# A fused two-layer block: the feed-forward's gate/up products rotate through six accumulator banks instead of eight, with three spare buffers instead of four

## The chip, the core and the metric

The kernel runs on one core of a Trainium2 chip. A core has TensorE (PE) for matrix products, VectorE (DVE), ScalarE (ACT) and GpSimd (POOL) for the rest, and SyncE (SP), whose queue issues the loads from HBM. They work side by side and wait for each other on semaphores. PE writes only to PSUM, an accumulator memory of 8 banks of 128 partitions by 512 float32 values; DVE and ACT read it from there. The metric is the device time of one execution in microseconds (us); less is better. Three executions of the kernel before took 1556.65, 1557.42 and 1561.18 us.

## The reference

A first block (gated delta rule and windowed attention, 256 tokens of width 1024) is followed by a second one of two layers. Each of these layers is a feed-forward, a mixer, and another feed-forward, each with its own modulated norm and gate:

```python
D_FF = 2816; HALF_STEP = 0.5

def _swiglu(h, w_gate, w_up, w_down):
    return (jax.nn.silu(h @ w_gate) * (h @ w_up)) @ w_down

for l in range(DEPTH_2):                                   # 2 layers
    mod = jax.nn.silu(c) @ w_mod[l] + b_mod[l]
    sh1, sc1, g1, sh2, sc2, g2, sh3, sc3, g3 = jnp.split(mod[:, None, :], N_MOD, axis=-1)
    h = _rmsnorm_2(x) * (1.0 + sc1) + sh1
    x = x + HALF_STEP * g1 * _swiglu(h, ffn1_w_gate[l], ffn1_w_up[l], ffn1_w_down[l])
    h = _rmsnorm_2(x) * (1.0 + sc2) + sh2
    x = x + g2 * _hybrid_mixer(h, w_in[l], w_out[l], ...)
    h = _rmsnorm_2(x) * (1.0 + sc3) + sh3
    x = x + HALF_STEP * g3 * _swiglu(h, ffn2_w_gate[l], ffn2_w_up[l], ffn2_w_down[l])
```

All is float32. The change touches the four feed-forwards and the places where they meet their neighbours.

## The kernel before

The program is written out by hand, engine by engine (`tensor_program`, `vector_program`, and so on). Nothing reorders it: each engine runs its list in order, and a `wait_ge(key)` stands where a step needs another's result. `Lane.wait_ge` leaves out a wait that an earlier one on the same engine already covers, since a semaphore only counts up.

**The feed-forward.** The four are called by (layer, sub): (0,0), (0,2), (1,0), (1,2). The hidden width of 2816 is 22 column blocks of 128, called f or x; they are taken in 11 pairs, which I number 0 to 10. For the precision, each float32 operand is split in a rounded high part and a low rest, and each product is the sum of high x high, high x low and low x high. A pair runs in four quarters q: gate weights with the first four slices of the model width, gate weights with the other four, then the same with the up weights. In each quarter PE does first the column block j = 0 of the pair, then j = 1 (`pe_ffn`). For each slice there is one product of 512 columns (`ps<-hh,whi`: the high weights against the high and low input side by side) and one of 256 (`ps<-hh,wlo`). A column block accumulates in two PSUM banks, one for gate and one for up, so a pair uses four banks. They are taken at q = 0, two when j = 0 begins and two when j = 1 begins, by `pe.bank(key, "ga")`.

**The banks.** `Tensor.bank` hands out the banks of a named pool in turn, and makes PE wait until the last holder of that bank is free. `POOLS` lists the pools: "ga" for gate/up, "down" for the four accumulators of the down product, "turnf" and "turnx" for the normed input that PE turns ahead of a block ("turnf" ahead of both mixers and of (1,0), "turnx" ahead of the others), "outx" for the mixer's output, "proj" (0, 1) and "rec" (2, 3) for the start of the mixer. The turn of "ga" is set back to 0 at the start of each feed-forward; with eight banks the even pairs use 0 to 3 and the odd ones 4 to 7.

**After the products.** When a column block is complete, ACT copies half of the two banks to a spare buffer (L2057, `copied`), DVE adds the other half (L2108, `summed`), and with that the two banks are free. ACT makes the Silu (L2060), DVE multiplies (L2113), ACT rounds the high part (L2064, `ahi`), POOL takes the low rest (L2076, `alo`). The spare buffers `SG` are the right halves of `H`, four of them, used in turn. In between ACT and DVE split the weight pieces of the next pair (L2026 `whi`, L2087 `wlo`); a piece can only be split when PE has done the piece four before it. In `split_all` the pieces of the next pair's quarters 0, 1 and 2 come ahead of the work on the finished pair, that of quarter 3 behind it.

**Beside it.** In the feed-forwards DVE also computes the modulation vectors of later stages: products with the vector c over tiles of 128 x 1024, summed (L555, `v_mods`), placed by `beside` and `along`. There is much of it in the first three feed-forwards and little in the last.

**The down product** takes its four banks all at once, before its first matmul, and then runs 22 slices of 12 matmuls. Then `v_join` scales by the gate, adds to x, and frees the banks; the norm and the turn-in of the next stage follow.

Of the kernel before, what the change touches and what calls it, by code (L numbers as in the profile page):

```python
# [107 lines left out]
ALU, ACT, AX = mybir.AluOpType, mybir.ActivationFunctionType, mybir.AxisListType  # L108
# [104 lines left out]
def plain(a):  # L213
    return a.bitcast(f32)


NS = 5
POOLS = {"all": range(8), "crow": (0, 1), "ccol": (2, 3), "tx": (4, 5, 6, 7), "six": range(6), "mods": (6, 7), "rest": (0, 1), "att": (2, 3, 4, 5), "bo": (7,), "sq": (4, 5, 6, 7), "low": (0, 1), "skk": (2,), "sdec": (4, 5), "sq2": (6, 7), "ga": range(8),
         "down": (4, 5, 6, 7), "chain": (2, 3, 4, 5), "proj": (0, 1), "rec": (2, 3), "sd": (4, 5, 6), "dbo": (7,), "outx": (2, 3, 0, 1), "ds": (4, 5, 6, 7), "turnf": (0, 1, 2, 3), "turnx": (6, 7, 4, 5)}


class Store:
# [203 lines left out]
class Tensor(Lane):  # L426
# [6 lines left out]
    def bank(self, key, pool="all"):  # L433
        banks = POOLS[pool]
        i = self.turn.get(pool, 0)
        self.turn[pool] = i + 1
        b = banks[i % len(banks)]
        if b in self.held:
            self.wait_ge(("free", self.held[b]))
        self.held[b] = key  # L440
        self.M.banks[key] = b
        return self.M.psum[:, b, :]
# [1482 lines left out]


def spare(M):
    return [M.H[:, 2 * i:2 * i + 2, 256:512] for i in range(4)]


def piece(M, i, n):

    return [t[:, i % 4, :].rearrange("p (a b) -> p a b", b=n) for t in (M.WHI, M.WLO)]


def pieces(l, sub):

    out, n = [], 0
    for f in range(0, 22, 2):
        for i in range(2):  # L1940
            for h in range(2):
                out.append((n, ("fw", l, sub, f, i), 4 * h, 4, 256, h == 1))
                n += 1
    for k0 in range(0, 22, 2):
        for h in range(2):
            out.append((n, ("out", ("d", l, sub), k0), h, 1, 1024, h == 1))
            n += 1
    return out
# [72 lines left out]
def act_piece(a, l, sub, p):  # L2021
    M = a.M
    n, key, r0, rn, wd_, _ = p
    hi, _ = piece(M, n, wd_)
    a.wait_ge(key, ("staged", l, sub, n - 4))
    a.done(a.e.activation(hi, M.slot(key)[:, r0:r0 + rn, :], ACT.Copy), ("whi", l, sub, n))  # L2026


def act_ffn(a, l, sub):
    M = a.M  # L2030
    SG = spare(M)

    def emit(p):
        act_piece(a, l, sub, p)

    def high(blk, half):
        k, t = slice(4 * half, 4 * half + 4), slice(blk * 128, blk * 128 + 128)
        a.wait_ge(("h", l, sub, blk, half))
        a.done(a.e.activation(M.HHI[:, k, t], M.H[:, k, t], ACT.Copy), ("hhi", l, sub, blk, half))

    first = pieces(l, sub)[:4]
    high(0, 0)
    act_modulated(a, l, sub, 0)
    high(0, 1)
    emit(first[1])
    high(1, 0)
    act_modulated(a, l, sub, 1)
    high(1, 1)
    for p in first[2:]:
        emit(p)  # L2050
    for f in split_all(a, l, sub, emit, None):
        pair = range(f, f + 2) if isinstance(f, int) else ()
        for x in pair:
            key = ("gu", l, sub, x)
            b = M.banks[key, 0]
            a.wait_ge(key, ("alo", l, sub, x - 4))
            a.done(a.e.activation(SG[x % 4], M.psum[:, b:b + 2, 256:512], ACT.Copy), ("copied", l, sub, x))  # L2057
        for x in pair:
            a.wait_ge(("summed", l, sub, x))
            a.done(a.e.activation(SG[x % 4][:, 0, :], SG[x % 4][:, 0, :], ACT.Silu), ("silu", l, sub, x))  # L2060
        for j, x in enumerate(pair):
            i = x % 4
            a.wait_ge(("act", l, sub, f + j))
            a.done(a.e.activation(M.AHI[:, f + j, :], SG[i][:, 0, :], ACT.Copy), ("ahi", l, sub, f + j))  # L2064


def pool_ffn(g, l, sub):
    M = g.M
    SG = spare(M)
    for half in range(2):  # L2070
        k = slice(4 * half, 4 * half + 4)
        g.wait_ge(("hhi", l, sub, 0, half))
        g.done(g.e.tensor_tensor(M.HLO[:, k, 0:128], M.H[:, k, 0:128], plain(M.HHI[:, k, 0:128]), ALU.subtract), ("hlo", l, sub, half))
    for f in range(22):
        g.wait_ge(("ahi", l, sub, f))
        g.op(g.e.tensor_tensor(M.ALO[:, f, :], SG[f % 4][:, 0, :], plain(M.AHI[:, f, :]), ALU.subtract), ("alo", l, sub, f))  # L2076


def v_ffn(v, l, sub, work):
    M = v.M  # L2080
    SG = spare(M)

    def emit(p):
        n, key, r0, rn, wd_, ends = p
        hi, lo = piece(M, n, wd_)
        v.wait_ge(("whi", l, sub, n), ("staged", l, sub, n - 4))
        v.done(v.e.tensor_tensor(lo, M.slot(key)[:, r0:r0 + rn, :], plain(hi), ALU.subtract), ("split", l, sub, n),  # L2087
             *([M.freed(key)] if ends else []))

    def low(half):  # L2090
        k, t = slice(4 * half, 4 * half + 4), slice(128, 256)
        v.wait_ge(("hhi", l, sub, 1, half))
        v.done(v.e.tensor_tensor(M.HLO[:, k, t], M.H[:, k, t], plain(M.HHI[:, k, t]), ALU.subtract), ("hlo", l, sub, half))  # L2093

    first = pieces(l, sub)[:4]
    emit(first[0])
    v_modulated(v, l, sub, 1)
    low(0)
    emit(first[1])
    low(1)  # L2100
    for p in first[2:]:
        emit(p)
    for f in split_all(v, l, sub, emit, work):
        for j in range(2 if isinstance(f, int) else 0):
            i, key = (f + j) % 4, ("gu", l, sub, f + j)
            b = M.banks[key, 0]
            v.wait_ge(("copied", l, sub, f + j))
            v.done(v.e.tensor_tensor(SG[i], SG[i], M.psum[:, b:b + 2, 0:256], ALU.add), ("summed", l, sub, f + j),  # L2108
                   ("free", (key, 0)), ("free", (key, 1)))
        for j in range(2 if isinstance(f, int) else 0):  # L2110
            i = (f + j) % 4
            v.wait_ge(("silu", l, sub, f + j))
            v.done(v.e.tensor_tensor(SG[i][:, 0, :], SG[i][:, 0, :], SG[i][:, 1, :], ALU.mult), ("act", l, sub, f + j))  # L2113


def pe_ffn(pe, l, sub):
    M = pe.M
    pe.turn["ga"] = 0
    for f in range(0, 22, 2):
        for q in range(4):  # L2120
            n = 2 * f + q
            hi, lo = piece(M, n, 256)
            k0 = 4 * (q % 2)
            pe.wait_ge(("split", l, sub, n), ("hlo", l, sub, q % 2))
            for j in range(2):
                c, key = slice(j * 128, j * 128 + 128), ("gu", l, sub, f + j)
                if q == 0:
                    for i in range(2):
                        pe.bank((key, i), "ga")
                b = M.ps((key, q // 2))  # L2130
                for kt in range(k0, k0 + 4):
                    low = lambda: pe.mm(b[:, 0:256], lo[:, kt - k0, c], M.HHI[:, kt, :], False, False)
                    if kt:
                        low()
                    ins = pe.mm(b, hi[:, kt - k0, c], M.HH[:, :, kt, :], kt == 0, kt == 7)
                    if kt == 0:
                        low()
                if q == 3 and j == 0:
                    pe.done(ins, key)
            pe.done(ins, ("staged", l, sub, n), *([key] if q == 3 else []))  # L2140
    bs = [[pe.bank(("d", l, sub, blk, hf), "down") for hf in range(2)] for blk in range(2)]
    for k0 in range(19):
        part = [k0] if k0 < 18 else [18, 19, 20, 21]
        pe.wait_ge(("alo", l, sub, part[-1]))
        for blk, kt, hf in [(0, k_, h_) for k_ in part for h_ in range(2)] + [(1, k_, h_) for h_ in range(2) for k_ in part]:
            n, c, s = 44 + kt, slice(blk * 128, blk * 128 + 128), slice(hf * 512, hf * 512 + 512)
            hi, lo = piece(M, n, 1024)
            pe.wait_ge(("split", l, sub, n))
            ins = pe.mm3(bs[blk][hf], (M.AHI[:, kt, c], M.ALO[:, kt, c]), (hi[:, 0, s], lo[:, 0, s]), kt == 0, kt == 21)
            if kt == 21 or (blk and hf):  # L2150
                pe.done(ins, *([("staged", l, sub, n)] if blk and hf else []), *([("d", l, sub, blk, hf)] if kt == 21 else []))
# [801 lines left out]
```

## Time and profile before

| | |
|---|---|
| median of three runs | 1557.42 us (1556.65 to 1561.18) |
| the profiled execution's own time | 1561.18 us |
| its span, first to last instruction | 1559.4 us |
| mean granted clock of TensorE | 0.969 of 2.4 GHz |
| busy: PE, DVE, ACT, POOL | 1466.9, 1017.5, 699.6, 298.0 us |
| share of PE in the chain that ended last | 80% |
| instructions | 18939 |

A row of the profile names a line of the kernel, the engine, the operation, and output<-inputs. L445 is `Tensor.mm`, through which all matmuls go, so they are told apart by their tiles: `hh,whi` and `hh,wlo` are gate/up, `whi,ahi`, `wlo,ahi` and `whi,alo` are down. PEld is the load of a matmul's stationary weights, which runs beside the matmul ahead of it. Matmuls overlap in the pipeline, so the distance between two starts is their pace, not their durations. Rows of DVE overlap by 0.08 us in the same manner.

### The profile page before, as it was taken

How to read it: one execution, taken by the hardware profiler on the slowest of the kernel's cores; microseconds unless marked ns; L12 is line 12 of the kernel's file. 1: busy time of each engine (PE TensorE's matmuls, PEld its weight loads, DVE VectorE, ACT ScalarE, POOL GpSimd, SP SyncE). 2: the span in 40 equal slices, each digit the busy share in tenths (PEclk: the TensorE clock that was granted, in tenths of full speed). 3: DMA queues.
4: the chain of work that ended last, by engine and by line, in shares of the span. 5: the costliest groups of instructions: out<-in, count | busy, mean ns of one | idle time of the engine just before them, and what ended most of it. 6: DMA issues, size and time to landing. Idle time of an engine off the chain costs nothing.

```text
span 1559.4 us, 18939 instructions
## 1 busy us (share of the span) xinstructions
PE 1466.9 (94%) x7424; PEld 1129.5 (72%) x7424; DVE 1017.5 (65%) x1531; ACT 699.6 (45%) x1116; POOL 298.0 (19%) x269
## 2 busy tenths in 40 slices
PE   6997999989889999999989999899999999999999
PEld 3546556646678888775578888788887865778887
DVE  4276684852568887346568886688884553776654
ACT  4425321152255653362355654466542631466552
POOL 0321255002211110043221110011100341311100
PEclk8998999998899999999999999999999999999999
DMA  9444234224258889332348988488895413478551
GB/s 384 162 142 139 95 131 179 91 108 149 86 188 294 299 325 365 109 118 94 108 141 283 318 308 317 134 284 293 318 357 167 134 63 108 135 240 260 180 198 55
DMA packets 159641, 306.41 MB, mean 196 GB/s; under 512 B 5952, under 2 KB 115776, under 8 KB 148672
## 3 DMA queue, kind: packets, MB, share of 16 engines
q1 hardware_dynamic: 159120, 304.93, 56.4%
q8 instruction: 58, 0.95, 0.3%
q10 hardware_dynamic: 432, 0.27, 0.1%
q14 instruction: 31, 0.25, 0.1%
HBM read 304.11 MB, written 1.08 MB: 196 GB/s over the span
## 4 chain that ended last, share of the span: by engine, by line
PE 80%; DVE 11%; ACT 6%; issue 1%; POOL 1%; DMA 1%; SPq 0%; DVEq 0%; ACTq 0%
PE ps L445 79%; PE ps L448 1%; DMA ring<-in_w_first_dram 1%; DVE H L1911 1%; DVE arena L1277 1%; DVE arena L1274 1%; ACT arena L1541 1%; DVE H L1860 0%; DVE misc L1574 0%; DVE arena L2726 0%; DVE arena L1263 0%; DVE H L1845 0%; DVE X L1851 0%; POOL arena L2465 0%; DVE ring L555 0%
## 5 line engine op out<-in xcount | busy, mean ns | idle before, releaser
L445 PE MATMUL ps<-hh,whi 128*128 128x512 f32 x1408 | 485.4, 399 | 6.1 <-DVE hh L2093 6.1
L2087 DVE TENSOR_TENSOR wlo<-ring,whi 128x1024 fp32r<-128x1024 f32 x264 | 321.8, 1231 | 149.7 <-ACT whi L2026 147.6
L2026 ACT ACTIVATE whi<-ring 128x1024 fp32r<-128x1024 f32 x264 | 274.2, 1055 | 227.2 <-PE ps L445 210.2
L445 PE MATMUL ps<-hh,wlo 128*128 128x256 f32 x1408 | 366.3, 281 | 0.0
L445 PEld LDWEIGHTS ps<-hh,whi 128*128 128x128 f32 x1408 | 252.9, 189 | 55.6 <-DVE hh L2093 7.0
L445 PEld LDWEIGHTS ps<-hh,wlo 128*128 128x128 f32 x1408 | 266.3, 189 | 16.6
L445 PE MATMUL ps<-ring,H 128*128 128x512 f32 (+1 forms) x544 | 238.4, 590 | 9.2 <-ACT arena L2228 5.6
L445 PEld LDWEIGHTS ps<-ring,H 128*128 128x128 f32 x544 | 104.0, 198 | 116.7 <-issue 101.0
L555 DVE SCALAR_TENSOR_TENSOR ring<-ring,cb 128x1024 f32<-128x1024 f32 x144 | 179.0, 1244 | 4.4 <-DMA ring<-in_mods_dram 4.0
L445 PE MATMUL ps<-H,ring 128*128 128x256 f32 (+1 forms) x576 | 160.1, 437 | 4.9 <-ACT arena L840 3.7
L2076 POOL TENSOR_TENSOR alo<-H,ahi 128x256 fp32r<-128x256 f32 x88 | 70.5, 802 | 460.3 <-ACT ahi L2064 456.8
L445 PEld LDWEIGHTS ps<-arena 128*128 128x128 f32 (+3 forms) x1320 | 124.3, 171 | 36.3 <-issue 21.0
L445 PE MATMUL ps<-arena 128*128 128x64 f32 (+6 forms) x1320 | 138.2, 267 | 10.3 <-DVE arena L1588 7.4
L445 PEld LDWEIGHTS ps<-H,ring 128*128 128x128 f32 x576 | 111.2, 195 | 50.1 <-issue 32.1
L445 PE MATMUL ps<-whi,alo 128*128 128x512 f32 x376 | 145.2, 390 | 0.0
L445 PE MATMUL ps<-wlo,ahi 128*128 128x512 f32 x360 | 140.1, 389 | 0.0
L445 PE MATMUL ps<-whi,ahi 128*128 128x512 f32 x352 | 137.0, 389 | 0.0
L445 PEld LDWEIGHTS ps<-whi,alo 128*128 128x128 f32 x376 | 70.6, 188 | 14.9
L445 PEld LDWEIGHTS ps<-wlo,ahi 128*128 128x128 f32 x360 | 67.6, 188 | 14.2
L445 PEld LDWEIGHTS ps<-whi,ahi 128*128 128x128 f32 x352 | 66.1, 188 | 13.7
L2057 ACT ACTIVATE H<-ps 128x512 f32<-128x512 f32 x88 | 52.8, 600 | 48.6 <-PE ps L445 48.6
L2108 DVE TENSOR_TENSOR H<-H,ps 128x512 f32<-128x512 f32 x88 | 57.8, 680 | 5.0 <-ACT H L2057 3.8
(344 smaller groups left out, 1553.4 us busy)
## 6 DMA issues: line engine op xcount, KB each, us to landing
ring<-in_mods_dram SPq DMA_DIRECT2D x76, 1024.0 KB, 5.6
ring<-in_w_in_dram SPq DMA_DIRECT2D x48, 1024.0 KB, 5.2
ring<-in_ffn_w_gate_dram SPq DMA_DIRECT2D x44, 1024.0 KB, 5.4
ring<-in_ffn_w_up_dram SPq DMA_DIRECT2D x44, 1024.0 KB, 7.1
ring<-in_ffn_w_down_dram SPq DMA_DIRECT2D x44, 1024.0 KB, 6.4
ring<-in_w_out_dram SPq DMA_DIRECT2D x12, 1024.0 KB, 5.0
ring<-in_w_first_dram SPq DMA_DIRECT2D x8, 1024.0 KB, 14.3
gates<-gate_rows SPq DMA_DIRECT2D x7, 512.0 KB, 6.0
```

The costliest lines, as they stand in the source:

```text
L445: return self.e.matmul(o, lhsT, rhs, start=start, stop=stop)
L448: return self.e.transpose(o, in_, self.M.C["ident"])
L555: v.done(v.e.scalar_tensor_tensor(tile, tile, 1.0, M.cvec[p.k], ALU.mult, ALU.mult, accum_out=sums[:, j:j + 1]), ("mod sums", p.n), *([M.f ...
L1274: v.op(v.e.tensor_tensor(t, M.AT[:, k, 0:k].unsqueeze(2).broadcast_to([128, k, w_]), M.XS[:, k, k:32].unsqueeze(1).broadcast_to([128, k, w ...
L1277: v.op(v.e.tensor_tensor(x, x, t, ALU.add))
L1541: a.done(a.e.activation(sm[:, t4, :], sm[:, t4, :], ACT.Exp, bias=nm[:, t4:t4 + 1], accum_out=den[:, t4:t4 + 1]), ("soft", u))
L1911: v.done(v.e.tensor_scalar(M.H[:, k, blk * 128:(blk + 1) * 128], M.ps(key)[:, HS[k]], m[:, cc + k:cc + k + 1], m[:, cs + k:cs + k + 1], AL ...
L2026: a.done(a.e.activation(hi, M.slot(key)[:, r0:r0 + rn, :], ACT.Copy), ("whi", l, sub, n))
L2057: a.done(a.e.activation(SG[x % 4], M.psum[:, b:b + 2, 256:512], ACT.Copy), ("copied", l, sub, x))
L2076: g.op(g.e.tensor_tensor(M.ALO[:, f, :], SG[f % 4][:, 0, :], plain(M.AHI[:, f, :]), ALU.subtract), ("alo", l, sub, f))
L2087: v.done(v.e.tensor_tensor(lo, M.slot(key)[:, r0:r0 + rn, :], plain(hi), ALU.subtract), ("split", l, sub, n), *([M.freed(key)] if ends els ...
L2108: v.done(v.e.tensor_tensor(SG[i], SG[i], M.psum[:, b:b + 2, 0:256], ALU.add), ("summed", l, sub, f + j), ("free", (key, 0)), ("free", (key ...
```

## The change

The pool "ga" has six banks, 0 to 5, and its turn is no longer set back, so that a feed-forward starts where the one before it stopped (a feed-forward takes 44 banks). "down" is (2, 3, 4, 5) instead of (4, 5, 6, 7). "turnf" is (6, 7, 0, 1) instead of (0, 1, 2, 3). The spare buffers are three, and ACT's copy of block x waits for the low part of x - 3.

```diff
--- before.py
+++ after.py
@@ -215,8 +215,8 @@
 
 
 NS = 5
-POOLS = {"all": range(8), "crow": (0, 1), "ccol": (2, 3), "tx": (4, 5, 6, 7), "six": range(6), "mods": (6, 7), "rest": (0, 1), "att": (2, 3, 4, 5), "bo": (7,), "sq": (4, 5, 6, 7), "low": (0, 1), "skk": (2,), "sdec": (4, 5), "sq2": (6, 7), "ga": range(8),
-         "down": (4, 5, 6, 7), "chain": (2, 3, 4, 5), "proj": (0, 1), "rec": (2, 3), "sd": (4, 5, 6), "dbo": (7,), "outx": (2, 3, 0, 1), "ds": (4, 5, 6, 7), "turnf": (0, 1, 2, 3), "turnx": (6, 7, 4, 5)}
+POOLS = {"all": range(8), "crow": (0, 1), "ccol": (2, 3), "tx": (4, 5, 6, 7), "six": range(6), "mods": (6, 7), "rest": (0, 1), "att": (2, 3, 4, 5), "bo": (7,), "sq": (4, 5, 6, 7), "low": (0, 1), "skk": (2,), "sdec": (4, 5), "sq2": (6, 7), "ga": range(6),
+         "down": (2, 3, 4, 5), "chain": (2, 3, 4, 5), "proj": (0, 1), "rec": (2, 3), "sd": (4, 5, 6), "dbo": (7,), "outx": (2, 3, 0, 1), "ds": (4, 5, 6, 7), "turnf": (6, 7, 0, 1), "turnx": (6, 7, 4, 5)}
 
 
 class Store:
@@ -1925,7 +1925,7 @@
 
 
 def spare(M):
-    return [M.H[:, 2 * i:2 * i + 2, 256:512] for i in range(4)]
+    return [M.H[:, 2 * i:2 * i + 2, 256:512] for i in range(3)]
 
 
 def piece(M, i, n):
@@ -2053,13 +2053,13 @@
         for x in pair:
             key = ("gu", l, sub, x)
             b = M.banks[key, 0]
-            a.wait_ge(key, ("alo", l, sub, x - 4))
-            a.done(a.e.activation(SG[x % 4], M.psum[:, b:b + 2, 256:512], ACT.Copy), ("copied", l, sub, x))
+            a.wait_ge(key, ("alo", l, sub, x - 3))
+            a.done(a.e.activation(SG[x % 3], M.psum[:, b:b + 2, 256:512], ACT.Copy), ("copied", l, sub, x))
         for x in pair:
             a.wait_ge(("summed", l, sub, x))
-            a.done(a.e.activation(SG[x % 4][:, 0, :], SG[x % 4][:, 0, :], ACT.Silu), ("silu", l, sub, x))
+            a.done(a.e.activation(SG[x % 3][:, 0, :], SG[x % 3][:, 0, :], ACT.Silu), ("silu", l, sub, x))
         for j, x in enumerate(pair):
-            i = x % 4
+            i = x % 3
             a.wait_ge(("act", l, sub, f + j))
             a.done(a.e.activation(M.AHI[:, f + j, :], SG[i][:, 0, :], ACT.Copy), ("ahi", l, sub, f + j))
 
@@ -2073,7 +2073,7 @@
         g.done(g.e.tensor_tensor(M.HLO[:, k, 0:128], M.H[:, k, 0:128], plain(M.HHI[:, k, 0:128]), ALU.subtract), ("hlo", l, sub, half))
     for f in range(22):
         g.wait_ge(("ahi", l, sub, f))
-        g.op(g.e.tensor_tensor(M.ALO[:, f, :], SG[f % 4][:, 0, :], plain(M.AHI[:, f, :]), ALU.subtract), ("alo", l, sub, f))
+        g.op(g.e.tensor_tensor(M.ALO[:, f, :], SG[f % 3][:, 0, :], plain(M.AHI[:, f, :]), ALU.subtract), ("alo", l, sub, f))
 
 
 def v_ffn(v, l, sub, work):
@@ -2102,20 +2102,19 @@
         emit(p)
     for f in split_all(v, l, sub, emit, work):
         for j in range(2 if isinstance(f, int) else 0):
-            i, key = (f + j) % 4, ("gu", l, sub, f + j)
+            i, key = (f + j) % 3, ("gu", l, sub, f + j)
             b = M.banks[key, 0]
             v.wait_ge(("copied", l, sub, f + j))
             v.done(v.e.tensor_tensor(SG[i], SG[i], M.psum[:, b:b + 2, 0:256], ALU.add), ("summed", l, sub, f + j),
                    ("free", (key, 0)), ("free", (key, 1)))
         for j in range(2 if isinstance(f, int) else 0):
-            i = (f + j) % 4
+            i = (f + j) % 3
             v.wait_ge(("silu", l, sub, f + j))
             v.done(v.e.tensor_tensor(SG[i][:, 0, :], SG[i][:, 0, :], SG[i][:, 1, :], ALU.mult), ("act", l, sub, f + j))
 
 
 def pe_ffn(pe, l, sub):
     M = pe.M
-    pe.turn["ga"] = 0
     for f in range(0, 22, 2):
         for q in range(4):
             n = 2 * f + q
```

The instructions on each engine and their order stay the same, and only what they wait for changes. The first place is PE in (0,0), at the start of the gate/up products of pair 1; the names are the input's high and low parts (`hh`) and the weights' high and low parts (`whi`, `wlo`). Before:

```order
L445 MATMUL ps<-hh,whi 128x512 [waits s_act_done,s_dve_done]
L445 MATMUL ps<-hh,wlo 128x256 x2
L445 MATMUL ps<-hh,whi 128x512
L445 MATMUL ps<-hh,wlo 128x256
L445 MATMUL ps<-hh,whi 128x512
L445 MATMUL ps<-hh,wlo 128x256
L445 MATMUL ps<-hh,whi 128x512 x2
L445 MATMUL ps<-hh,wlo 128x256 x2
```

The same rows after the change:

```order
L445 MATMUL ps<-hh,whi 128x512 [waits s_act_done,s_dve_done]
L445 MATMUL ps<-hh,wlo 128x256 x2
L445 MATMUL ps<-hh,whi 128x512
L445 MATMUL ps<-hh,wlo 128x256
L445 MATMUL ps<-hh,whi 128x512
L445 MATMUL ps<-hh,wlo 128x256
L445 MATMUL ps<-hh,whi 128x512
L445 MATMUL ps<-hh,whi 128x512 [waits s_dve_done]
L445 MATMUL ps<-hh,wlo 128x256 x2
```

The first matmul of column block j = 1 of the pair now waits for DVE. Before, there was no wait at that place: the next one came with the second quarter.

The second place is PE in (0,2), from the end of the first slice of the down product to the beginning of the second (`ahi`, `alo`: the hidden activations). Before:

```order
L445 MATMUL ps<-wlo,ahi 128x512
L445 MATMUL ps<-whi,alo 128x512
L445 MATMUL ps<-whi,ahi 128x512 [waits s_dve_done,s_pool_done]
L445 MATMUL ps<-wlo,ahi 128x512
L445 MATMUL ps<-whi,alo 128x512
```

The same rows after the change:

```order
L445 MATMUL ps<-wlo,ahi 128x512
L445 MATMUL ps<-whi,alo 128x512
L445 MATMUL ps<-whi,ahi 128x512 [waits s_pool_done]
L445 MATMUL ps<-wlo,ahi 128x512
L445 MATMUL ps<-whi,alo 128x512
```

The second slice doesn't wait for DVE any more, because the wait in front of the first slice (for the banks) is now for a later step of DVE, which covers the split of the second slice's weights too.

## Rows read from the trace of the kernel before

**Rows 1.** The page: busy time by engine, and POOL's low parts.
```profile
PE 1466.9 (94%) x7424; PEld 1129.5 (72%) x7424; DVE 1017.5 (65%) x1531; ACT 699.6 (45%) x1116; POOL 298.0 (19%) x269
...
L2076 POOL TENSOR_TENSOR alo<-H,ahi 128x256 fp32r<-128x256 f32 x88 | 70.5, 802 | 460.3 <-ACT ahi L2064 456.8
```

**Rows 2.** The chain of waits: start, us, what; first and last feed-forward.
```profile
446.67 184.27 PE ps L445 x962
...
1371.41 184.10 PE ps L445 x968
```

**Rows 3.** Windows: us, busy by engine (PE, PEld, DVE, ACT, POOL), granted clock, DMA.
```profile
446.70:571.00 124.30, 124.30 (x698) 107.94 (x699) 103.65 (x142) 75.53 (x109) 14.79 (x20) 0.99 0.84 289
...
700.00:716.00 16.00, 13.59 (x76) 9.57 (x75) 12.60 (x15) 6.51 (x10) 8.48 (x7) 1.00 0.38 129
806.00:811.00 5.00, 3.40 (x16) 3.21 (x16) 3.27 (x7) 2.98 (x6) 2.17 (x2) 0.66 0.43 150
1371.40:1495.00 123.60, 123.59 (x702) 107.39 (x703) 84.89 (x104) 74.16 (x109) 14.76 (x20) 1.00 0.70 229
```

**Rows 4.** Timeline (start, us), all engines, end of (0,0)'s last pair.
```profile
572.00 0.19 PEld L445 LDWEIGHTS ps<-whi,ahi 128*128 128x128 f32 x1
572.23 0.40 PE L445 MATMUL ps<-whi,ahi 128*128 128x512 f32 x1
...
572.43 0.60 ACT L2057 ACTIVATE H<-ps 128x512 f32<-128x512 f32 x1 [0.82 <-PE ps L445]
...
573.05 1.28 DVE L2108 TENSOR_TENSOR H<-H,ps 128x512 f32<-128x512 f32 x2
```

**Rows 5.** Timeline, all engines, from (0,0)'s pair 9 into pair 10.
```profile
561.17 0.60 ACT L2057 ACTIVATE H<-ps 128x512 f32<-128x512 f32 x1 [0.82 <-PE ps L445]
561.19 1.30 DVE L2108 TENSOR_TENSOR H<-H,ps 128x512 f32<-128x512 f32 x2
...
562.02 0.30 PEld L445 LDWEIGHTS ps<-hh,whi 128*128 128x128 f32 x2
562.13 0.62 PE L445 MATMUL ps<-hh,whi 128*128 128x512 f32 x2
...
562.86 0.42 ACT L2064 ACTIVATE ahi<-H 128x256 fp32r<-128x256 f32 x1
```

**Rows 6.** Timeline, all engines, start of (0,0)'s gate/up products.
```profile
445.92 0.69 DVE L2093 TENSOR_TENSOR hh<-H,hh 128x512 fp32r<-128x512 f32 x1 [0.69 <-ACT hh L2039]
...
446.67 0.19 PEld L445 LDWEIGHTS ps<-hh,whi 128*128 128x128 f32 x1 [2.14 <-DVE hh L2093]
446.67 0.50 PE L445 MATMUL ps<-hh,whi 128*128 128x512 f32 x1 [1.95 <-DVE hh L2093]
446.77 0.42 PEld L445 LDWEIGHTS ps<-hh,wlo 128*128 128x128 f32 x2
```

**Rows 7.** Timeline, DVE and ACT, first and last pair with late additions.
```profile
458.10 1.23 DVE L2087 TENSOR_TENSOR wlo<-ring,whi 128x1024 fp32r<-128x1024 f32 x1 [1.63 <-ACT whi L2026]
...
459.77 0.60 ACT L2057 ACTIVATE H<-ps 128x512 f32<-128x512 f32 x1 [0.82 <-PE ps L445]
...
460.38 1.28 DVE L2108 TENSOR_TENSOR H<-H,ps 128x512 f32<-128x512 f32 x2
...
1405.51 0.60 ACT L2057 ACTIVATE H<-ps 128x512 f32<-128x512 f32 x1 [0.82 <-PE ps L445]
...
1406.13 1.27 DVE L2108 TENSOR_TENSOR H<-H,ps 128x512 f32<-128x512 f32 x2
```

**Rows 8.** Timeline, ACT and DVE, last pairs of (1,0) and (1,2).
```profile
1129.73 0.60 ACT L2057 ACTIVATE H<-ps 128x512 f32<-128x512 f32 x1 [0.82 <-PE ps L445]
...
1130.35 1.28 DVE L2108 TENSOR_TENSOR H<-H,ps 128x512 f32<-128x512 f32 x2
...
1495.12 0.68 DVE L2108 TENSOR_TENSOR H<-H,ps 128x512 f32<-128x512 f32 x1
...
1495.64 0.60 ACT L2057 ACTIVATE H<-ps 128x512 f32<-128x512 f32 x1 [0.82 <-PE ps L445]
```


## The prediction

> **What bounds the kernel now.** I read the page first: TensorE (PE) is busy for 1466.9 of 1559.4 us, and no other engine comes near it [rows 1]. Then the chain of waits, where the reader is to see one thing: each of the four feed-forward blocks is a single unbroken piece of PE work. The first runs for 184.27 us from 446.67, the last for 184.10 us from 1371.41 [rows 2], and the two between them look the same. Together that is some 737 us with nothing in between, so a stall of PE inside a block is added to the end in full, and no idle time exists there that could give it back. The windows by stage say the same: PE is busy for 124.30 of 124.30 us in the first gate/up half and for 123.59 of 123.60 in the last, at granted clock 0.99 and 1.00 [rows 3].
>
> Then the timeline around the place where a pair of blocks of the hidden width ends, since the change moves the waits there. I write E for the start of the second ACT copy of a pair (L2057, waits for PE's last matmul of the pair). In the last pair of (0,0), E is 572.43. PE goes on without a gap: the weight load of the first down matmul is at 572.00 and the matmul at 572.23, so E - 0.43 and E - 0.20 [rows 4]. One pair earlier E is 561.17, 11.26 us before. Half a quarter later PE turns to the second column block of the next pair; the two weight loads in a row mark it (562.02 and 562.13) and the second of the two matmuls in a row, at 562.37: so E + 0.96 and E + 1.20 [rows 5].
>
> **The change part by part.**
>
> *The six-bank ring.* A pair takes four banks. With eight banks a pair needs those of the pair two before it, freed long ago. With six, the first block of a pair takes banks of the pair before last, but the second block takes the two that the first block of the pair just finished has held. So once per pair PE must wait, at E + 0.96, for DVE's addition to that block (L2108, "summed"), and this wait stood nowhere near the path before. When is the addition done? DVE's row x2 holds both additions of a pair; a single one takes 0.68 us [rows 8], so the first one is over 0.68 us after the row's start.
> - In the pair that ends at 572.43 the row starts at 573.05 (`v_ffn` runs a modulation product, L555, just ahead of it): over at 573.73, E + 1.30 [rows 4].
> - In the pair that ends at 561.17 it starts at 561.19: over at E + 0.70 [rows 5], 0.26 us before the weight load is due. No stall.
> - In the last feed-forward block, once the modulation work has run out, it is over at E + 0.16 [rows 8]. No stall.
>
> The late kind is every second pair of the first three blocks (pairs 0, 2, 4, 6, 8) and pairs 0 and 2 of the last: 17 pairs, the first with E 459.77 and the row at 460.38, the last with E 1405.51 and the row at 1406.13, both E + 0.61 + 0.68 = E + 1.29 to 1.30 [rows 7]. It doesn't get less late when PE has been held up: the DVE row that opens its chain sat idle for 1.63 us for ACT's rounded weight piece, which itself waits for PE's third quarter of the same pair [rows 7]. So the lateness moves along with PE and is paid each time.
>
> What does a wait cost that ends late? At the start of the feed-forward block DVE's row ends at 446.61; weight load and matmul begin at 446.67, and with the next weight load at 446.77 the first matmul streams from there [rows 6]. So streaming starts 0.15 us after the end of the awaited row. A late pair: E + 1.30 + 0.15 against E + 1.20, 0.25 us. 17 x 0.25 = 4.3 us. The trace has no wait of PE in mid-stream that just misses, so this is bounded: from below 0.10 us less (the weight load not held by the wait), 0.15 us, 2.6 us in all; from above 0.23 us more (a further weight load that can't run ahead, the 0.23 between load and matmul in rows 4), 0.48 us, 8.2 us in all. I take 0.25, the row nearest in kind. Below nothing is excluded, since PE has no idle time in these stretches.
>
> *The down banks and the ring without a reset.* A block takes 44 banks, 44 mod 6 is 2, so the four blocks start at banks 0, 2, 4 and 0. Down now takes banks 2 to 5 at once, before its first matmul. In (0,0) and (1,2) the last pair holds 4, 5 (first column block) and 0, 1: down waits for the first addition. In (0,2) and (1,0) its second column block holds 2, 3 and 4, 5: down waits for the second addition. Before, down had 4 to 7, held by the pair before. The matmul was due at E - 0.20:
> - (0,0): E + 1.30 + 0.15 + 0.20 = 1.65 us [rows 4].
> - (0,2) and (1,0): the second addition is over at 1131.63 with E at 1129.73, so E + 1.90 [rows 8]; 1.90 + 0.35 = 2.25 us each. The pairs of (0,2) have the same rhythm.
> - (1,2): the first addition is over at 1495.80, E 1495.64 [rows 8]; 0.16 + 0.35 = 0.51 us.
>
> Sum 6.7 us; by the same bounds (0.10 less, 0.23 more, four times) 6.3 to 7.6.
>
> *Three spare buffers instead of four.* ACT's copy of block x now waits for the low part of x - 3, not x - 4. For the first of a pair that lies two pairs back, for the second in the first half of the pair before. ACT rounds the first block of a pair at 562.86, E + 1.69 [rows 5], and POOL's 0.80 us [rows 1] follow; the copy that now waits comes 9.8 us after E. Nothing; if that cover were gone, a delay of ACT would first eat the slack of the additions above.
>
> *Turn-in banks.* The mixers and (1,0) now turn in to 6, 7, 0, 1. 6 and 7 are idle in the gate/up half and 0, 1 are freed by its last pairs at the latest, a whole down product earlier. The mixer's first projections take bank 0 and 1, now held by the second row block's turn-in; but they need that block's modulated rows anyway. Nothing. No instruction is added, removed or put elsewhere on any engine, DMAs included.
>
> The sum: 4.3 + 6.7 = 11.0 us. The profiled execution has span 1559.4 and time 1561.18; with the change 1570.4 and 1572.2. The median of the runs shown, 1557.42, lies 3.8 us under the profiled one, so the forecast of the median is 1557.4 + 11.0 = 1568.4.
>
> **The rivals.** A measurement of this kernel can tell about 0.3% (4.7 us) from no change: up to 1562.1 counts as the same.
>
> *Only the four down starts cost.* If the late additions in mid-block are taken up (DVE's row ends are no release times, and the gap to cover is 0.25 us), 6.7 us stay: 1564.1. For it: the miss is small. Against it: the weight load is due at E + 0.96, and the addition only starts at E + 0.61 and has 0.68 us to run.
>
> *The clock falls.* Stalls of 2 us in the middle of a dense stream could bring PE to its lower level, 1.2 GHz. In 806 to 811, after a join in which PE sat idle at several places, the granted clock is 0.66: 5 x 0.34 / 0.5 = 3.4 us at half speed. If that followed each of four down starts, PE at half speed for 3.4 us would lose 1.7 us each time: 6.8 more, 1575.2. Against it: from 700 to 716 PE is busy for 13.59 of 16.00 us, idle for 2.41, more than any stall forecast here, and the clock stays at 1.00 [rows 3]. The Trainium skill, "TensorE: Matmul & The Clock Gate", section "A second HAM failure mode: psum-queue depth-cycling", speaks for this rival: a kernel that cycled through its PSUM banks idled so often in short gaps between groups that the clock went back and forth, at a cost in throughput though single matmuls looked alike. By that rule, with gaps at each late pair too, the time would lie at this rival's or above; this trace shows no such case, as its ring never stalled.
>
> *The waits are hidden.* The change does in the program what it says, but if PE's waits for the additions released by other means (the row ends being late by 2 us) it would give 1557.4.
>
> *Faster.* PE spends 11.26 us on a pair of 32 matmuls of 512 and 32 of 256 columns; at 2.4 GHz these columns are 10.24 us. The other 1.02 us a pair, 45 us over 44 pairs, could be a collision of PE's reads with what ACT and DVE move in SBUF and PSUM. If the smaller set of banks and buffers took a third of it away, 15 us, the time would be 1557.4 + 11.0 - 15 = 1553.4; it decides from 11.0 us, a pair under 11.01 us between stalls. Against it: the excess doesn't depend on that traffic. The first block's gate/up half has DVE busy for 103.65 us and the last one's for 84.89, with DMA shares 0.84 and 0.70 [rows 3], and the blocks take 184.27 and 184.10 us [rows 2].
>
> **How the numbers follow.** Forecast 0.64; only the down starts 0.16; clock 0.08; hidden 0.07; faster 0.05. The predicted time is the forecast's, 1568.4. Its own range is 8.9 to 15.8 us over the median, 1566.3 to 1573.2. Low end of the range: the down starts alone with 2 us of scatter, 1562. High end: 1574. Slower by over 0.3%: 0.64 + 0.08 + most of 0.16 = 0.85. Same: 0.07 and the rest, 0.10. Faster: 0.05.
>
> **What would show it.** In the profile after: (a) PE rows with idle time before them, released by DVE L2108 (the addition), some 17 of 0.2 to 0.5 us at E + 0.96 in mid-pair, in every second pair, and four at the first down matmul, about 1.6, 2.2, 2.2 and 0.5 us; (b) the three middle blocks' pieces in the chain broken by ACT and DVE, and the blocks 187.2, 187.6, 187.6 and 185.1 us long; (c) mixers and joins unchanged; (d) clock 1.00 in the blocks. The forecast is wrong if the PE rows wait for the additions but resume sooner than 0.15 us, if odd pairs stall as well (then 0.26 us of slack was no slack), or if the clock in the blocks falls under 0.98.

## The result, and the profile after

The changed kernel takes 1571.41 us (median of 4 runs, 1570.06 to 1571.86) against 1558.26 for the kernel before beside it: 13.2 us slower, ratio 1.0088, 95% interval 1.0072 to 1.0105. The forecast was 11.0 us slower, 1568.4. (One execution of the kernel before, beside later runs, took 1706.64 us at a granted clock of 0.823; no comparison here uses it.) The profiled execution has a span of 1573.8 us, 14.4 over the 1559.4 of before. By the page's first line PE is busy for 6.9 us more, its weight loads for 3.1, and the others for the same within 0.7:

```profile
PE 1473.8 (94%) x7424; PEld 1132.6 (72%) x7424; DVE 1018.1 (65%) x1531; ACT 699.0 (44%) x1116; POOL 297.8 (19%) x269
```

The view of waits shows where the time went. PE's matmul rows waited five times for DVE's addition (L2108), but the rows of the weight loads did so 21 times; in the kernel before neither did once:

```profile
PE ps L445 <- DVE H L2108: 5.9, 5, 2.0
...
PEld ps L445 <- DVE H L2108: 12.4, 21, 2.3
```

21 is 17 + 4. Why the matmul rows show so few is seen in the timeline (all engines) of a late pair, (0,0)'s pair 0, which answers to [rows 7] and [rows 5]:

```profile
459.82 0.60 ACT L2057 ACTIVATE H<-ps 128x512 f32<-128x512 f32 x1 [0.82 <-PE ps L445]
...
460.44 1.28 DVE L2108 TENSOR_TENSOR H<-H,ps 128x512 f32<-128x512 f32 x2
...
460.79 0.89 PE L445 MATMUL ps<-hh,whi 128*128 128x512 f32 x2
...
461.18 0.19 PEld L445 LDWEIGHTS ps<-hh,whi 128*128 128x128 f32 x1 [0.31 <-DVE H L2108]
461.29 0.42 PEld L445 LDWEIGHTS ps<-hh,wlo 128*128 128x128 f32 x2
461.52 0.40 PE L445 MATMUL ps<-hh,wlo 128*128 128x256 f32 x2
```

E is 459.82. The addition is over at 460.44 + 0.68 = 461.12, and the load starts 0.06 us later, at 461.18, where it was due at 460.78. The matmuls of 512 columns are drawn as one row of 0.89 us (0.62 in [rows 5]), since their ends are modelled: the hole is in there. Start to start tells it: 461.52 less 460.79 is 0.73, where the same stretch before took 0.47 (460.73 to 461.20).

The end of (0,0)'s last pair, as in [rows 4] (timeline, all engines):

```profile
573.75 0.60 ACT L2057 ACTIVATE H<-ps 128x512 f32<-128x512 f32 x1 [0.81 <-PE ps L445]
...
574.37 1.28 DVE L2108 TENSOR_TENSOR H<-H,ps 128x512 f32<-128x512 f32 x2
...
575.11 0.19 PEld L445 LDWEIGHTS ps<-whi,ahi 128*128 128x128 f32 x1 [1.72 <-DVE H L2108]
575.11 0.50 PE L445 MATMUL ps<-whi,ahi 128*128 128x512 f32 x1 [1.40 <-DVE H L2108]
```

The chain of waits, one piece from 446.67 before [rows 2], is broken there, and shows what sets the addition's time (start, us, what):

```profile
446.75 124.15 PE ps L445 x688
...
570.99 1.07 ACT whi L2026
...
572.08 1.23 DVE wlo L2087
573.31 1.14 DVE ring L555 x2
574.45 0.61 DVE H L2108
...
575.11 58.79 PE ps L445 x258
```

PE's third quarter releases ACT's rounding, this DVE's rest, then comes the modulation product, then the addition. The chain leaves the block's matmuls at 633.90, six before the last, as it did before: 187.15 us against 184.27, forecast 187.2.

In (0,2) something more is to be seen. PE's rows at the start of down (timeline):

```profile
942.00 0.50 PE L445 MATMUL ps<-whi,ahi 128*128 128x512 f32 x1 [1.99 <-DVE H L2108]
942.33 0.39 PE L445 MATMUL ps<-wlo,ahi 128*128 128x512 f32 x1
942.56 0.47 PE L445 MATMUL ps<-whi,alo 128*128 128x512 f32 x1
942.83 0.63 PE L445 MATMUL ps<-whi,ahi 128*128 128x512 f32 x1
943.26 0.63 PE L445 MATMUL ps<-wlo,ahi 128*128 128x512 f32 x1
943.69 0.63 PE L445 MATMUL ps<-whi,alo 128*128 128x512 f32 x1
```

From 942.83 on the starts are 0.43 us apart instead of 0.23: PE is at its lower clock. The windows (columns as in [rows 3]; the granted clock is third from the end) show it behind the stalls of (0,2) and (1,0), at the start of (1,0), and not in the last block (the start of (0,0), not shown, has it in both kernels):

```profile
942.70:946.20 3.50, 3.50 (x10) 2.69 (x9) 2.67 (x4) 1.39 (x3) 3.25 (x2) 0.51 0.18 53
1013.50:1018.00 4.50, 4.43 (x14) 3.85 (x15) 4.02 (x5) 3.21 (x5) 0.00 (x0) 0.52 0.55 167
1144.10:1147.60 3.50, 3.50 (x10) 2.75 (x9) 2.01 (x3) 1.28 (x2) 2.81 (x2) 0.51 0.51 130
1384.70:1509.00 124.30, 124.27 (x703) 107.54 (x704) 85.11 (x105) 74.14 (x109) 14.75 (x20) 1.00 0.69 228
```

**The sum of the profiled execution**, from the distances between matmul starts. Of each block I take first gate/up start to last down start; without a stall and at full clock that is 183.7 us.

| block | before | after | mid-pair waits | down start | rest |
|---|---|---|---|---|---|
| (0,0) | 185.2 | 188.1 | 1.27 | 1.66 | 1.5 |
| (0,2) | 183.7 | 188.9 | 1.46 | 2.25 | 1.5 |
| (1,0) | 183.7 | 190.5 | 1.27 | 2.30 | 3.3 |
| (1,2) | 183.7 | 184.7 | 0.50 | 0.51 | 0.0 |
| all | 736.4 | 752.3 | 4.50 | 6.7 | 6.2 |

The waits are 11.2 us. The rest is the lower clock: matmul starts 0.43 us apart. The kernel before has 1.5 us of it in its blocks, this one 6.2. 11.2 + 4.7 is 15.9; outside the blocks the execution lost 1.5 us less than that of before, which makes the 14.4.

### The profile page after: what moved, and what is told of

Its sections match the earlier page's. It is cut to its first block, busy times and chain, and to the rows that moved or that the text cites. A ratio compares the mean times of both kernels' runs of the same rounds, so it can differ in the third digit from the quotient of the medians.

```text
span 1573.8 us, 18934 instructions
## 1 busy us (share of the span) xinstructions
PE 1473.8 (94%) x7424; PEld 1132.6 (72%) x7424; DVE 1018.1 (65%) x1531; ACT 699.0 (44%) x1116; POOL 297.8 (19%) x269
## 4 chain that ended last, share of the span: by engine, by line
PE 77%; DVE 12%; ACT 6%; DMA 2%; issue 2%; POOL 1%; SPq 0%; DVEq 0%; ACTq 0%
PE ps L445 76%; PE ps L448 1%; DMA ring<-in_w_first_dram 1%; DVE H L1911 1%; DVE ring L555 1%; DVE arena L1277 1%; DVE arena L1274 1%; DMA ring<-in_ffn_w_gate_dram 1%; DVE wlo L2087 1%; ACT arena L1541 1%; ACT whi L2026 0%; DVE H L1860 0%; DVE misc L1574 0%; DVE H L2108 0%; DVE arena L2725 0%
## 5 line engine op out<-in xcount | busy, mean ns | idle before, releaser
L445 PE MATMUL ps<-hh,whi 128*128 128x512 f32 x1408 | 490.8, 401 | 5.9 <-DVE hh L2093 5.7
L2108 DVE TENSOR_TENSOR H<-H,ps 128x512 f32<-128x512 f32 x88 | 58.2, 682 | 7.8 <-ACT H L2057 7.4
## 6 DMA issues: line engine op xcount, KB each, us to landing
ring<-in_w_first_dram SPq DMA_DIRECT2D x8, 1024.0 KB, 13.5
```

What stands on the lines that cost most here:

```text
L445: return self.e.matmul(o, lhsT, rhs, start=start, stop=stop)
```

## The experiments

Theory W: the time is PE's waits for the additions, plus what the clock does. Rivals: the spare buffers or turn-in banks cost something; six banks cost something by themselves. Differences are medians against the kernel before on the same chip; where a diff is against the changed kernel it says so. `POOLS` entries are shown alone.

**Spares and turn-in banks alone.** The changed kernel, with the ring and down as before:

```diff
-"ga": range(6)   "down": (2, 3, 4, 5)
+"ga": range(8)   "down": (4, 5, 6, 7)
 def pe_ffn(pe, l, sub):
+    pe.turn["ga"] = 0
```

> The three spare buffers and the new turn-in banks alone; gate/up keeps eight banks with the reset, down keeps 4 to 7. Theory W (the time is made of PE's waits for DVE's additions and of what the clock does after them): no wait is added on PE, 0 us, within 0.3% of the kernel before; the four blocks 185.2, 183.7, 183.7, 183.7 us from first gate/up matmul to last down matmul, as before. Rival S (the fourth buffer's loss delays ACT's copies, or the turn-in banks hold up the mixers): 2 us or more slower, with ACT's copy row waiting for POOL.

1560.49 against 1561.20 us, ratio 0.9994 (0.9984 to 1.0004); no load or matmul waits for L2108, and three of the four blocks take 183.6 to 183.7 us (the fourth, 185.0, has the lower clock at its start). These two parts add no wait, and rival S, 2 us or more, falls.

**Only the mid-pair waits.** The changed kernel, with

```diff
-"down": (2, 3, 4, 5)
+"down": (6, 7, 2, 3)
 def pe_ffn(pe, l, sub):
+    pe.turn["ga"] = 0
```

> The whole change, but the ring starts at bank 0 in each block and down takes 6, 7, 2, 3, which are free by then: only the mid-pair waits stay. Theory W: 17 late pairs at 0.25 us, 4.3 us slower than before (about 1562.5 if before is 1558.3), no half-clock stretch inside a block. Rival (the mid-pair waits cost little and the down starts make the 13 us): under 2 us slower. Rival (short gaps in mid-block also bring the clock down): over 8 us slower, with matmul starts 427 ns apart after some of them.

1566.80 against 1561.20: 5.6 us, ratio 1.0043 (1.0029 to 1.0058). The waits of its profile:

```profile
PEld ps L445 <- DVE H L2108: 5.3, 17, 0.3
```

Seventeen, and by matmul starts they cost 4.3 us: 0.145 us until the late matmul and 0.10 at the next, 0.25 each, as Theory W has it. The median lies above that, the interval from 4.5 to 9.1 us; the profile has 2.1 us of lower clock at the start of (0,2). There is no lower clock in mid-block: the 17 short holes didn't bring it down here.

**Only down starts, on the second addition.** The kernel before, with

```diff
-"down": (4, 5, 6, 7)
+"down": (2, 3, 4, 5)
```

> The kernel before, with down on banks 2 to 5: each of the four down starts waits for the second addition of the last pair, no other wait is added. Theory W with the clock: four stalls of 2.25, 2.25, 2.25 us and, in the last block, 1.33 + 0.35 = 1.7 us, 8.4 us together, and behind each of the three long ones a stretch at 1.2 GHz that costs 1.7 us, 5.1 us: 13.5 us slower. Theory W without the clock (what the profile of the changed kernel shows of it is chance): 8.4 us slower.

1570.88 against 1561.20: 9.7 us, ratio 1.0062 (1.0046 to 1.0079). Four waits:

```profile
PEld ps L445 <- DVE H L2108: 8.7, 4, 2.3
```

By starts they cost 2.25, 2.25, 2.25 and 1.67 us, 8.4 as forecast. The windows behind the first and the third of the stalls, alike in length:

```profile
571.90:576.00 4.10, 4.10 (x18) 3.40 (x19) 3.19 (x5) 3.09 (x5) 3.18 (x2) 1.00 0.33 93
...
1136.70:1140.30 3.60, 3.55 (x9) 2.80 (x10) 3.17 (x5) 2.12 (x4) 2.60 (x2) 0.53 0.42 98
```

The same stall left the clock at 1.00 once and brought it to 0.53 once. So the clock doesn't answer every stall of 2.2 us, and it does so in other kernels than the changed one too. The median, 9.7, lies between the theory's two numbers.

**Only down starts, on the first addition.** The kernel before, with

```diff
-"down": (4, 5, 6, 7)
+"down": (0, 1, 4, 5)
```

> The kernel before, with down on banks 0, 1, 4, 5: each down start waits for the first addition of the last pair. Theory W: stalls of 1.65 us three times and 0.51 us, 5.5 us slower. If the clock falls only behind the longer stalls, as in (0,2) and (1,0) of the changed kernel and not in its (0,0), no more than that; if it falls behind these too, 1.7 us for each of three, 10.6 us slower.

1564.94 against 1561.20: 3.7 us, ratio 1.0022 (1.0011 to 1.0033).

```profile
PEld ps L445 <- DVE H L2108: 5.7, 4, 1.7
```

The stalls cost 1.65, 1.65, 1.66 and 0.50 us in the profile, 5.5 as forecast; the median came out 1.8 lower, its interval just short of it. The clock behind them is 1.00, (0,0) shown:

```profile
573.90:577.00 3.10, 3.10 (x14) 2.55 (x14) 2.66 (x6) 2.53 (x5) 1.62 (x1) 1.00 0.37 152
```

**The changed kernel again.**

> The changed kernel once more, beside three variants of it. Theory W: 11.0 us of waits, plus a stretch at 1.2 GHz worth 1.7 us behind those of the two stalls of 2.2 us (down starts of (0,2) and (1,0)) that the clock happens to answer: between 11 and 14.4 us slower than before. If such a stretch stood behind both stalls in every execution, always 14.4; in the run that broke the stalls apart (down on banks 2 to 5), one of three stalls of 2.2 us was followed by one.

1572.72 against 1559.50: 13.2 us, ratio 1.0084 (1.0072 to 1.0097). Its profile has 4.5 + 6.7 us of waits again, half-clock stretches behind both stalls of 2.2 us again, and none at the start of (1,0): 4.6 us of lower clock in the blocks instead of 6.2.

**The ring set back.** The changed kernel, with

```diff
 def pe_ffn(pe, l, sub):
     M = pe.M
+    pe.turn["ga"] = 0
```

> The changed kernel with the ring set back to bank 0 in each block, so that every down start waits for the first addition of the last pair, none for the second. Theory W: 4.3 us in mid-pair as before, and 1.65, 1.65, 1.65 and 0.51 us at the down starts, 5.5 us: 9.7 us slower than the kernel before, 1.2 us and the clock's share (up to 3.4) less than the changed kernel; no stretch of matmul starts 427 ns apart behind a down start. Rival (the clock falls by chance behind any down stall): the stretches stay and the time is within 1 us of the changed kernel's.

> The changed kernel with the ring set back, again: its first five rounds gave 13.9 us over the kernel before where its waits are worth 9.7. Theory C: 9.3 to 9.8 us of waits in the profile again, the rest half-clock stretches at block starts, in another number than the three of its first profile; median between 9.7 and 15 us over before. Rival (a cost of the reset itself): the same blocks longer by the same amount.

1573.44 against 1559.50 and, again, 1571.78 against 1559.68: 13.9 and 12.1 us, ratios 1.0092 (1.0077 to 1.0107) and 1.0084 (1.0065 to 1.0103). The waits are as forecast in both, 9.8 and 9.9 us, and no stretch at the lower clock follows a down start. But the gain on the changed kernel that Theory W promised doesn't show in the medians: the first is within 1 us of the changed kernel's beside it, as the rival had it, though the stretches that the rival needed aren't there. The lower clock is at the block starts instead. Windows of the first 5 us of (0,2), in the first and in the second profile:

```profile
812.50:817.90 5.40, 5.40 (x19) 4.63 (x20) 4.10 (x4) 3.25 (x6) 0.00 (x0) 0.57 0.58 194
```

```profile
812.60:817.90 5.30, 5.30 (x30) 4.67 (x31) 4.81 (x5) 4.18 (x6) 0.00 (x0) 1.00 0.54 195
```

The first profile has it at the starts of (0,0), (0,2) and (1,0), 5.1 us, the second at those of (0,0) and (1,2), 3.1 us: it differs between executions of one program.

**The kernel before again.**

> The kernel before once more, for a second profile of it. Theory C (where the half-clock stretches behind the joins fall against the starts of the feed-forward blocks differs from one execution to the next, and each that reaches into a block costs 1 to 2 us there): the blocks are 183.7 us but for 0 to 2 of the four, which are 1 to 2 us longer at their start; the granted clock in mid-block is 1.00 throughout. Rival (such stretches come with the changed code alone): the same single one, at (0,0), as in the first profile.

1559.18 against 1559.68. One block of four has the stretch, now (1,0) and not (0,0):

```profile
444.90:450.00 5.10, 5.10 (x30) 4.46 (x31) 4.61 (x5) 4.13 (x6) 0.00 (x0) 1.00 0.59 196
...
1001.70:1007.00 5.30, 5.30 (x22) 4.59 (x23) 4.04 (x4) 3.79 (x6) 0.00 (x0) 0.68 0.58 198
```

That fits Theory C. What it leaves open: before, its rerun and the first experiment have one such start each, the others between one and four (longer blocks shift where the joins fall), and one profile each can't tell this from luck.

**The product put behind the additions.** The changed kernel, with

```diff
 def beside(f, q):
-    return 2 if q == 3 else 1
+    return (1, 1, 0, 3)[q]
```

> The changed kernel with the modulation product that DVE makes ahead of the late additions put behind them (none in a pair's third quarter, up to one more in the fourth). Theory W: the additions are over by E + 0.7 at the latest, so no mid-pair stall is left (17 before); down starts 0.51 us in (0,0) and (1,2) and, for the second addition at E + 1.32, 1.67 us in (0,2) and (1,0): 4.4 us slower than the kernel before. Rival (PE stalls because DVE is busy as a whole, not because of this order): 8 us or more slower, since DVE's work is the same.

1567.09 against 1559.50: 7.6 us, ratio 1.0045 (1.0033 to 1.0057). Theory W's 4.4 lies outside the interval (5.1 to 8.9 us), the rival's 8 inside it.

```profile
PEld ps L445 <- DVE H L2108: 8.1, 11, 2.3
```

Seven mid-pair waits are left, not none: by the timeline of the first of them, the products put behind one pair's additions keep DVE busy without a pause up to the next pair's, which start 1.46 us after E. In (0,2) it still reaches the last addition late and down waits 2.2 us. By matmul starts the waits are 2.5 us in mid-pair and 5.0 at the down starts, 7.5 us, so the waits do account for the median; what was wrong is where the forecast saw DVE free. Moving the work helps and doesn't cure.

**Both cures.** The version with free down banks, with the same edit of `beside`:

> Both cures together: ring of six set back to 0, down on banks 6, 7, 2, 3, and the modulation product behind the additions. Theory W: PE waits for no addition anywhere; within 0.3% of the kernel before, blocks 185.2 and 183.7 us from first gate/up to last down matmul but for a half-clock stretch at a start. Rival (six banks cost something by themselves, such as collisions, beside the waits): 3 us or more slower with no gap between matmul starts that explains it.

1564.19 against 1559.50: 4.7 us, ratio 1.0029 (1.0017 to 1.0041).

```profile
PEld ps L445 <- DVE H L2108: 2.8, 7, 1.1
```

The seven waits cost 2.4 us; the profile has the lower clock at all four block starts (6.5 us), and no other gap. The "waits for no addition anywhere" of the forecast was wrong in the same place as above.

**More late additions.** The version with free down banks, with

```diff
 def beside(f, q):
-    return 2 if q == 3 else 1
+    return (1, 1, 2, 1)[q]
```

> The ring of six with free down banks (only mid-pair waits), and one more modulation product's turn ahead of the additions, so that late additions come in nearly every pair of the first three blocks: some 33 instead of 17. Theory W: each costs 0.25 us, 8.3 us of mid-pair stalls in the profile where the version with 17 has 4.3; median 4 us over that version's, 8 to 10 us over before. Rival (a wait costs by how late it is, and the additions get later too): over 12 us.

1573.19 against 1559.68: 13.5 us, ratio 1.0087 (1.0070 to 1.0105).

```profile
PEld ps L445 <- DVE H L2108: 13.3, 33, 0.9
```

33 waits as counted. Those of the even pairs cost 0.25 us each again, but the new ones 0.33 to 0.82, since they come with longer busy stretches of DVE: 11.4 us by matmul starts, not 8.3. A wait costs its own lateness plus 0.10: here the rival, over 12 us in the median, was right and the flat 0.25 us for each wait wrong.

**The late banks needed later.** The version with free down banks; from the second pair on PE does both gate quarters of the first column block, then both of the second:

```diff
-        for q in range(4):
...
-            for j in range(2):
+        for qs in ((0, 1), (2,), (3,)) if f else ((0,), (1,), (2,), (3,)):
+            for j in range(2):
+                for q in qs:
...
```

> The ring of six with free down banks, and PE does both gate quarters of the first column block of a pair before the second block's (from the second pair on), so that the two banks that come late are needed 1.4 us later. Theory W: the addition is over at E + 1.30, the load is now due at E + 2.37, so no stall at all; blocks 183.7 us but for the clock at their starts, within 0.3% of before. Rival (the later release of the first weight piece holds up the splits): gaps between matmul starts in the third or fourth quarter, 3 us or more slower.

1561.25 against 1559.68: 1.6 us, ratio 1.0014 (1.0002 to 1.0025). No row of any kind waits for L2108, and the block of (0,2) is a single piece of the chain again, 0.4 us shorter than before's:

```profile
809.47 183.72 PE ps L445 x968
```

The profile has the lower clock at two block starts (3.1 us). So six banks and three spares cost nothing in waits once the late banks are asked for 1.4 us later. The median isn't lower for the shorter blocks (1.7 us over all four): the two starts cost 1.6 us more than the one in the profile of before, and the rest is not shown. No version here beats the kernel before.

## Why the prediction was right, and where it fell short

The direction and the mechanism held, step by step:

- *No cover.* PE's blocks had no idle time, and every wait was added in full: the four blocks grew by 15.9 us, 11.2 of waits and 4.7 of lower clock, and the span by 14.4.
- *The six-bank ring.* 17 late pairs: 17 waits in the profile, and 0 in the odd pairs. 0.25 us each: 0.25 (0.145 + 0.10), 4.3 us; a second profile gave the same. One pair in (0,2) cost 0.2 us more in both profiles of the changed kernel. The chain (at the last pair) shows the late addition hanging on PE's own third quarter, which was the reason that the lateness repeats.
- *The down banks.* Forecast 1.65, 2.25, 2.25, 0.51; measured 1.66, 2.25, 2.30, 0.51.
- *Spares and turn-in banks.* Nothing forecast, -0.7 us measured (-2.5 to +0.6 by the ratio); the estimate at equal clock, below, doesn't exclude 1 us.
- *What the profile would show.* I expected PE rows with idle time before them. Five came; the other sixteen holes lie inside modelled matmul durations, and only the weight loads' rows show them. The clock of 1.00 in the blocks didn't come: it was 0.99, 0.99, 0.98 and 1.00, and (0,2) and (1,0) grew by 5.2 and 6.8 us from first to last matmul start where 3.5 each was forecast.

The step that fell short was the clock: I gave this rival 0.08 and priced it as a case of its own, against a window (700 to 716, [rows 3]) in which PE was idle for 2.41 us at clock 1.00. That window was misread: the idle time is one wait that ends at 715.82, 0.18 us before the window does, so it can't show what the clock does behind it. The same wait stands in the second mixer, up to 1274.05, and there the trace of the kernel before has the clock down (windows):

```profile
1271.00:1280.00 9.00, 6.59 (x22) 4.13 (x22) 7.16 (x13) 2.54 (x4) 2.05 (x2) 0.81 0.07 25
```

A clock of 0.81 over 9 us is 3.4 us at half speed. In the 14 profiles this wait of 2.4 us comes 28 times, and a stretch at the lower clock begins within 1.5 us of its end 5 times. Over the seven profiles of kernels with down stalls, it came behind 5 of 8 stalls of 2.2 us (both of each profile of the changed kernel, 1 of 3 on the second addition, 0 of 1 with the early additions), and behind none of 13 of 1.65 to 1.68 us. It costs 1.5 to 1.6 us each time, where I had 1.7. At that rate two stalls of 2.2 us are worth 2 us (an estimate), and the likeliest case should have been 13.0 us instead of 11.0, which lies just under the measured interval (11.2 to 16.4 us). In the Trainium skill, "TensorE: Matmul & The Clock Gate", section "A second HAM failure mode: psum-queue depth-cycling", short gaps between groups bring the clock back and forth; here 17 gaps of 0.3 us didn't and the longer ones at the down starts did in 5 of 8 cases, so its rule held for a part of the stalls only.

One more reading was wrong without harm. The pieces of 184.27 and 184.10 us in [rows 2], given against the rival "faster", aren't alike: the first leaves out the block's last six matmuls and holds the lower clock of its start. From first to last start the blocks take 185.2 and 183.7 us. In the second profile of the kernel before, (0,0) takes 183.7 us too, so the argument stands.

What isn't settled is the clock at the starts of the blocks. The waits alone would put the version with the ring set back at 9.8 us; its medians are 13.9 and 12.1. Its profiles, like that of the last experiment, which has no wait, show more in-block time at the lower clock (3.0 to 5.1 us) than the kernel before (1.5 in each of two). The record lets one go a step further, since it has the span and the mean granted clock of every execution. They go together: with the ring set back, the fastest execution took 1567.5 us at 0.973 and the slowest 1576.5 at 0.963. Over 185 executions of all versions, a line with one slope (0.86 us for each 0.001 of clock) follows an execution's distance from its own version's mean, with a standard deviation of 1.0 us about the line where it was 2.2 without. By that slope, and so an estimate, the versions at equal clock lie over the kernel before by:

| version | waits in the profile | at equal clock, 95% |
|---|---|---|
| changed kernel | 11.2 | 12.5 (0.5 either way) |
| ring set back | 9.8 | 11.3 (0.6) |
| only mid-pair waits | 4.3 | 5.5 (0.6) |
| down on the first addition | 5.5 | 5.5 (0.6) |
| late banks needed later | 0 | 0.0 (0.6) |
| spares and turn-in banks alone | 0 | 0.8 (0.6) |

So the 1.4 us that setting back the ring should save are there (1.2, 0.7 either way), hidden in the medians by a lower clock, 0.9693 on average against 0.9709 for both the changed kernel and the kernel before. Whether a shift of the joins by a few us makes it lower, or luck does, was not tried apart, and some 1 us of the changed kernel's cost is in neither the waits nor the clock; the spare buffers and turn-in banks may hold a part of it. It bounds what the medians can tell: single terms were read from distances between matmul starts, not from medians, which lie up to 2 us below and 4 us above the waits.

## What to carry to other kernels

A ring of buffers is deep enough when its oldest holder is free before the engine that sets the pace asks for it, and this is to be checked against the latest release in the trace, not a typical one: here every second one was late, at 0.25 us each, and an engine without idle time pays it each time. Where a buffer comes late, asking for it later (1.4 us was enough) cured it, while moving the other engine's work about took away 10 of 17 waits and left 7. Before a stall is priced by its length, look for the clock behind it, in a window that begins where the stall ends, and at every place where the trace has such a stall.

## What the runs showed of the hardware

- A stall of PE of 2.2 us at the start of down brought the granted clock to 0.51 to 0.53 for some 3.5 us in 5 of 8 cases, a wait of 2.4 us in the mixers in 5 of 28, and stalls of 1.65 to 1.68 us in 0 of 13.
- A weight load that waits for a DVE row starts 0.05 to 0.07 us after that row's end, and the stream goes on another 0.10 us late (load at 461.18, next load at 461.29).
- A hole of 0.25 us between matmuls doesn't show in the matmul rows: in the version with mid-pair waits alone, 17 of 17 were seen only before weight loads.
- Executions of one kernel differ in time mostly as their mean granted clock does: 0.86 us for each 0.001, over 185 executions.
- With the two gate quarters done one after the other for a column block, a block of 968 matmuls took 183.2 to 183.3 us from first to last start instead of 183.7, at the same clock of 1.00 ((0,2) and (1,0)).
